# The DeltaNet inverse of a hybrid decoder trunk: fills regrouped, transposes as fills, the last level interleaved

## The reference

```python
A = jnp.where(strict, jnp.einsum('nbhid,nbhjd->nbhij', kb, kc) * decay, 0.0)
T = lax.linalg.triangular_solve(eye + A, jnp.broadcast_to(eye, A.shape), left_side=True, lower=True)
u = T @ vb
w = T @ (kb * jnp.exp(g)[..., None])
...
def step(state, xs):
    v_new = u_i - w_i @ state
    o = (q_i * jnp.exp(g_i)[..., None]) @ state + a_i @ v_new
    ...
```

## Time and profile before

| what | value |
|---|---|
| median of three runs | 1017.67 us (1017.45 to 1018.24) |
| the profiled execution, its own time | 1018.01 us |
| span of its instructions | 1016.2 us |
| PE busy | 1004.5 us (99%) |
| DVE busy | 727.6 us (72%) |
| ACT busy | 602.1 us (59%) |
| POOL busy | 254.7 us (25%) |
| mean granted clock of PE | 0.997 |

### The profile page before, as it was taken

How to read it: one execution, slowest core, us unless ns; L and a number is a source line. 1 busy time by engine, 2 the same in 40 slices (tenths; PEclk the granted TensorE clock), 3 DMA queues, 4 the chain that set the end, 5 groups by cost and what they waited for, 6 DMA issues and landing times.

```text
span 1016.2 us, 19037 instructions
## 1 busy us (share of the span) xinstructions
PE 1004.5 (99%) x6450; PEld 881.3 (87%) x6450; DVE 727.6 (72%) x1206; ACT 602.1 (59%) x1097; POOL 254.7 (25%) x275
## 2 busy tenths in 40 slices
PE   9999999999999999999999999999999999999996
PEld 7888888899988888888888888889999888888885
DVE  5776666899787866666786666668987977666666
ACT  6555555777566655555675555558675575555554
POOL 2767222100520122222202222220016102222221
PEclk9999999999999999999999999999999999999998
DMA  7966666485224666666637666656832338666651
GB/s 230 269 208 201 187 192 193 131 232 165 81 65 125 191 207 192 195 187 188 205 127 223 187 188 194 195 153 170 226 118 64 91 99 272 197 191 188 190 180 42
DMA packets 249882, 176.27 MB, mean 173 GB/s; under 512 B 5875, under 2 KB 235400, under 8 KB 249832
## 3 DMA queue, kind: packets, MB, share of 16 engines
q1 hardware_dynamic: 248800, 174.35, 56.9%
q0 software_dynamic: 400, 0.91, 0.4%
q10 hardware_dynamic: 632, 0.34, 0.1%
HBM read 174.53 MB, written 1.05 MB: 173 GB/s over the span
## 4 chain that ended last, share of the span: by engine, by line
PE 95%; DVE 3%; ACT 1%; issue 0%; DVEq 0%; POOL 0%; POOLq 0%; ACTq 0%
PE bank L800 27%; PE bank L804 14%; PE bank L771 13%; PE bank L772 13%; PE bank L773 13%; PE bank L787 3%; PE bank L790 1%; PE bank L811 1%; PE bank L846 1%; PE bank L1192 1%; PE bank L1179 1%; PE bank L1122 1%; PE bank L853 1%; PE bank L881 0%; PE bank L1104 0%
## 5 line engine op out<-in xcount | busy, mean ns | idle before, releaser
L1894 DVE TENSOR_TENSOR Wl<-raw,Wh 128x1024 fp32r<-128x1024 f32 x324 | 401.8, 1264 | 52.8 <-ACT Wh L1428 52.5
L1428 ACT ACTIVATE Wh<-raw 128x1024 fp32r<-128x1024 f32 x323 | 321.9, 1048 | 19.9 <-PE bank L773 18.0
L800 PE MATMUL bank<-X,Wh 128*128 128x512 f32 x1216 | 288.3, 389 | 0.0
L800 PEld LDWEIGHTS bank<-X,Wh 128*128 128x128 f32 x1216 | 227.9, 188 | 47.2
L623 POOL TENSOR_TENSOR gact<-gact,pooled 128x256 f32<-128x256 f32 x85 | 63.6, 748 | 535.0 <-DVE gact L1993 525.6
L804 PEld LDWEIGHTS bank<-X,Wl 128*128 128x128 f32 x1216 | 153.9, 189 | 5.8
L804 PE MATMUL bank<-X,Wl 128*128 128x256 f32 x1216 | 155.7, 281 | 0.0
L771 PE MATMUL bank<-Wh,aH 128*128 128x512 f32 x336 | 132.4, 394 | 0.2
L772 PE MATMUL bank<-Wl,aH 128*128 128x512 f32 x336 | 131.8, 392 | 0.0
L773 PE MATMUL bank<-Wh,aL 128*128 128x512 f32 x336 | 130.8, 389 | 0.0
L1560 ACT ACTIVATE aH<-hid 128x256 fp32r<-128x256 f32 x84 | 35.1, 418 | 149.1 <-DVE hid L2008 149.1
(11 more groups left out here) (325 smaller groups left out, 1355.6 us busy)
## 6 DMA issues: line engine op xcount, KB each, us to landing
raw<-in_ffn_w_gate SPq DMA_DIRECT2D x88, 512.0 KB, 4.6
raw<-in_ffn_w_up SPq DMA_DIRECT2D x88, 512.0 KB, 3.7
raw<-in_ffn_w_down SPq DMA_DIRECT2D x88, 512.0 KB, 3.3
raw<-in_w_in SPq DMA_DIRECT2D x48, 512.0 KB, 4.8
raw<-in_w_out SPq DMA_DIRECT2D x16, 512.0 KB, 3.3
xr<-in_x SPq DMA_DIRECT2D x2, 512.0 KB, 4.1
out_x<-big SPq DMA_DIRECT2D x3, 256.0 KB, 2.6
cst<-in_consts POOLq DMA_DIRECT2D x1, 688.0 KB, 4.8
```

The lines of the kernel that those rows point to most:

```text
L800: nc.tensor.matmul(b[:, :], piece(Wh, 3 * par + j)[:, k, :], X[:, k, :, :], start=k == 0, stop=False)
L1428: return nc.scalar.activation(Wh[:, s, 0:D_MODEL], raw[:, s, :], ACT.Copy).then_inc(hi_cast.sem, 1)
L1894: return nc.vector.tensor_tensor(low_at(s, skewed), raw[:, s, :], Wh[:, s, 0:D_MODEL].bitcast(F32), ALU.subtract).then_inc(lo_cast.sem, 1)
```

## The change

- PE: the fills are cut at the steps 4, 9, 14, 19 and 24 of the 24 steps. The first four steps come ahead of the first level, the transposes of `VT` come behind it as its fill (now into banks 0 and 1), and five steps each come behind the second, third and fourth level and the quarters. The first level's D no longer waits for the copies of `V`.
- PE: the last level runs as P of half 0, the transposes of q, P of half 1 alternating with D of half 0, the transposes of k, D of half 1. `half_d` reads the diagonal block from `DT`, not from `T64`.
- ACT: the copies of `V` come behind the first level's copies. The edges are written to `DT`, behind DVE's copies of the diagonal blocks. The copy of the pooling input comes ahead of the last level's copies, which alternate with `qT` and `kT`.
- DVE: the 128x4 product and the four copies to `DT` come ahead of the last level. The low cast of piece 27 comes behind the maxima of the first two attention heads.

```diff
-FILL_LEVELS = 2
+FILL_ENDS = (4, 9, 14, 19, 24)
...
-                for c in range(HALVES):
+                def turn_v():
                     pe.wait_ge(*conv_act.at(layer, 12))
-                    pe.wait_ge(*at_done.at(layer, c + 1))
-                    for h in range(DN_HEADS):
-                        m = nc.tensor.transpose(bank[6 + c][:, h * P:(h + 1) * P], VT[:, h, c * P:(c + 1) * P], ident)
-                    m.then_inc(v_turned.sem, 1)
+                    for c in range(HALVES):
+                        for h in range(DN_HEADS):
+                            m = nc.tensor.transpose(bank[c][:, h * P:(h + 1) * P], VT[:, h, c * P:(c + 1) * P], ident)
+                        m.then_inc(v_turned.sem, 1)
...
-                def turn_qk():
+                def turn_qk(j):
                     pe.wait_ge(*roped.at(layer, 4))
-                    for j in range(2):
...
+                    pe.wait_ge(*v_copied.at(layer, j + 1))
...
+                def fill(first, last):
+                    for step in range(first, last):
+                        n, k = divmod(step, KT)
...
                     pe.wait_ge(*pm_done.at(layer, 2 * n + c + 1))
-                    if n == 0:
-                        pe.wait_ge(*v_copied.at(layer, c + 1))
-                    else:
+                    if n:
                         pe.wait_ge(*dt_done.at(layer, 2 * (n - 1) + c + 1))
...
+                def half_level():
+                    pe.wait_ge(*d_done.at(layer, 8 + 1))
+                    for h, u in units(0):
+                        m = half_p(h, u)
                     m.then_inc(p_done.sem, 1)
+                    turn_qk(0)
+                    pe.wait_ge(*d_done.at(layer, 8 + 2))
+                    pe.wait_ge(*pm_done.at(layer, 10 + 1))
+                    pe.wait_ge(*dt_edge.at(layer, 1))
+                    for (h, u), (_, v) in zip(units(0), units(1)):
+                        p = half_p(h, v)
+                        d = half_d(h, u)
+                    p.then_inc(p_done.sem, 1)
+                    d.then_inc(dd_done.sem, 1)
+                    turn_qk(1)
+                    pe.wait_ge(*pm_done.at(layer, 10 + 2))
+                    pe.wait_ge(*dt_edge.at(layer, 2))
+                    for h, u in units(1):
+                        m = half_d(h, u)
                     m.then_inc(dd_done.sem, 1)
...
+                fill(0, FILL_ENDS[0])
                 for n in range(len(LEVELS)):
...
+                    if n == 0:
+                        turn_v()
+                    else:
+                        fill(FILL_ENDS[n - 1], FILL_ENDS[n])
+                for stage in (quarter_p, quarter_d):
+                    for c in range(HALVES):
+                        stage(c)
+                fill(FILL_ENDS[3], FILL_ENDS[4])
+                half_level()
...
-                    nc.scalar.activation(T64[0:32, u, 32:64], src[0:32, :, :], ACT.Copy)
-                    nc.scalar.activation(T64[64:96, u, 32:64], src[64:96, :, :], ACT.Copy).then_inc(dt_edge.sem, 1)
+                    act.wait_ge(*dt_joined.at(layer, c + 1))
+                    nc.scalar.activation(DT[0:32, u, 32:64], src[0:32, :, :], ACT.Copy)
+                    nc.scalar.activation(DT[64:96, u, 96:128], src[64:96, :, :], ACT.Copy).then_inc(dt_edge.sem, 1)
                 z_silu(3)
                 act.preload_act_table_set(LN_EXP)
+                pool_raw(0)
                 for c in range(HALVES):
+                    act.wait_ge(*qk_turned.at(layer, c + 1))
+                    nc.scalar.activation((qT, kT)[c][:, :, :].rearrange("p a t -> p (a t)"), bank[c][:, :],
+                                         ACT.Copy).then_inc(qk_copied.sem, 1)
                     act.wait_ge(*dd_done.at(layer, 10 + c + 1))
...
+                small(nc.vector.tensor_tensor(beta_dec, beta_k[:, 0:4], dec[:, 0:4, P - 1:P].rearrange("p u t -> p (u t)"),
+                                              ALU.mult))
+                dve.wait_ge(*cleared.at(layer, 1))
+                for c in range(HALVES):
+                    u = slice(4 * c, 4 * c + 4)
+                    dve.wait_ge(*dt_done.at(layer, 6 + c + 1))
+                    for q in BLOCKS:
+                        op = nc.vector.tensor_copy(DT[q, u, q], T64[q, u, :])
+                    op.then_inc(dt_joined.sem, 1)
                 for c in range(HALVES):
                     dve.wait_ge(*p_done.at(layer, 10 + c + 1))
...
                 lo_mix(layer, 26)
-                lo_mix(layer, 27)
...
                 maxima(1)
+                lo_mix(layer, 27)
```

More of the change, by code:

```diff
@@ L1136, in mixer @@
                 pe.wait_ge(*at_done.at(layer, 4))
-                def turn_qk():
+                def turn_qk(j):
                     pe.wait_ge(*roped.at(layer, 4))
-                    for j in range(2):
[L1142 to L1156, removed]
-                    else:
-                        pe.wait_ge(*pool_x.at(layer, 1))
-                    for k in ks:
+                    pe.wait_ge(*v_copied.at(layer, j + 1))
@@ new lines, in turn_qk @@
+                    for c in range(HALVES):
+                        for pair in range(2):
+                            m = nc.tensor.transpose(bank[j][:, pair * SEQ + c * P:pair * SEQ + (c + 1) * P],
+                                                    qkr[:, c, j * 256 + pair * P:j * 256 + (pair + 1) * P], ident)
+                    m.then_inc(qk_turned.sem, 1)
+                def fill(first, last):
+                    for step in range(first, last):
+                        n, k = divmod(step, KT)
+                        pos, out = FILL_POSITIONS[n], bank[(3, 2, 3)[n]][:, 0:SEQ]
+                        s = MIX_SLOTS[pos]
+                        if step == first or k == 0:
+                            split(pos)
+                            if pos == POS_POOL1:
+                                pe.wait_ge(*diff_done.at(layer, 2))
+                            elif pos == POS_Z3:
+                                pe.wait_ge(*z_act.at(layer, 3))
+                            else:
+                                pe.wait_ge(*pool_x.at(layer, 1))
@@ L1160, in fill_part @@
                         m = three(out, piece(Wh, s)[:, k, :], low_piece(s)[:, k, :], Xh[:, k, :], Xl[:, k, :],
                                   k == 0, k == KT - 1)
-                    if ks[-1] == KT - 1:
-                        m.then_inc(proj.sem, 1)
+                        if k == KT - 1:
+                            m.then_inc(proj.sem, 1)
                 def units(c):
@@ L1218, in quarter_d, with half_p @@
                     m.then_inc(dd_done.sem, 1)
[L1220 to L1225, removed]
-                    m.then_inc(p_done.sem, 1)
[L1228 to L1234, removed]
+                def half_p(h, u):
+                    return nc.tensor.matmul(bank[4 + u // DN_HEADS][HALF:, h * HALF:(h + 1) * HALF], LT[0:HALF, u, HALF:],
+                                            D64[0:HALF, u, :], start=True, stop=True)
@@ new lines, in half_d @@
+                def half_d(h, u):
+                    return nc.tensor.matmul(bank[6 + u // DN_HEADS][0:HALF, h * HALF:(h + 1) * HALF], PM[HALF:, u, 0:HALF],
+                                            DT[HALF:, u, HALF:], start=True, stop=True)
+                def half_level():
+                    pe.wait_ge(*d_done.at(layer, 8 + 1))
+                    for h, u in units(0):
+                        m = half_p(h, u)
+                    m.then_inc(p_done.sem, 1)
+                    turn_qk(0)
[12 more added lines that the diff above has]
+                        m = half_d(h, u)
@@ L1235, in half_d @@
                     m.then_inc(dd_done.sem, 1)
+                fill(0, FILL_ENDS[0])
                 for n in range(len(LEVELS)):
-                    k = 4 * (n % 2)
                     for stage in (level_p, level_d):
@@ L1315, in mixer @@
                 pe.wait_ge(*dt_edge.at(layer, 3))
-                pe.wait_ge(*dt_joined.at(layer, 1))
                 pe.wait_ge(*pm_done.at(layer, 2 * N_LEVELS))
@@ L1325, in mixer @@
                 pe.wait_ge(*dt_edge.at(layer, 4))
-                pe.wait_ge(*dt_joined.at(layer, 2))
                 pe.wait_ge(*vd_done.at(layer, 1))
@@ L1747, in mixer @@
                 z_silu(2)
[L1748 to L1752, removed]
                 for n, s in enumerate(LEVELS):
@@ L1758, in mixer @@
                         nc.scalar.activation(even, src, ACT.Copy).then_inc(d_done.sem, 1)
+                    if n == 0:
+                        act.wait_ge(*q_summed.at(layer, 2))
+                        for c in range(HALVES):
+                            act.wait_ge(*v_turned.at(layer, c + 1))
+                            nc.scalar.activation(V[:, 4 * c:4 * c + 4, :].rearrange("p u d -> p (u d)"), bank[c][:, :],
+                                                 ACT.Copy).then_inc(v_copied.sem, 1)
                     act.wait_ge(*k_norm.at(layer, 1))
@@ L1763, in mixer @@
```

(4 more changed lines are left out.)

## The result

The changed kernel takes 1019.17 us (median of 20 runs, 1018.28 to 1019.75), the kernel before 1017.43 us beside it (20 runs, 1016.79 to 1018.24): ratio 1.0016, 95% interval 1.0011 to 1.0022. It is slower, by 1.7 us and not by the 4.0 of the forecast. That is within the 0.2% that the forecast called no change, but the interval tells it from no change all the same. The profiled execution took 1018.93 us, with a span of 1017.1 us.

What follows compares the result with a forecast made beforehand. PE was taken as busy nearly throughout, so its work and new waits decide. Per layer +1.5 ahead of T and +0.5 behind, twice +2.0 is +4.0 on 1018.01, less 0.34 for the median: 1021.7 us, range 1017.6 to 1023.2.

Steps and rivals of the forecast that it cites:

- First level, -0.20: First level of the inverse on PE: D no longer waits for V's copies, 1.25 becomes 1.05 us behind P.
- PE's own order in full: PE's work in the inverse, if nothing else holds it: first product with DT at 288.06 instead of 288.36.
- +0.86: Quarters on PE: 19 fill steps ahead instead of 16 make them 1.06 us later, less 0.20 from the first level.
- -0.1: Last level on PE: three blocks of 0.79, 2.37 us, against 2.45 before; bounds -0.3 to +0.4.
- T: Start of the first product that uses the finished inverse DT, at 288.36 us in layer 0 of the kernel before.
- The middle block's 0.60: Last level on PE: alternating P and D run together as pairs, in the time of one half, 0.60 us.
- The way of the blocks to DT, +1.8 on top of that: DVE's copies wait for POOL's steps, three waits of 0.6; T at 289.9, +1.5 per layer against before (-0.3 to +2.3).
- the small product, 0.57: DVE's small product between the quarters' negations and the copies to DT: claimed to take 0.57 us.
- ACT from the last copy to T, 3.8: ACT's edges, activation, table load, pooling copy, qT and DT block: 3.71 us, about 3.8 with a semaphore.
- A copy waits for POOL: DVE's copies to DT: each waits for the POOL step it meets, and POOL's next step for it; at most 2.6 us.
- Behind T, +0.5: Low cast of piece 27 behind the maxima: L2378 0.8 us later, 0.3 absorbed, 0.5 per layer carried on (bounds 0 and 0.8).
- the first rival: Copies to DT run beside POOL unhindered: T at 288.1, +0.24 per layer, 1018.2 us; chance 0.22.

Runs made afterwards that it cites:

- the run with POOL held: Changed kernel with POOL's first windows made to wait until DVE's four copies to DT are done: 1017.98 us, ratio 1.0007.
- the run with the cast alone: Kernel before with only the low cast of piece 27 moved behind the maxima: 1018.58 us, ratio 1.001.

## Why the prediction was wrong

The mechanism was right and its size was not. By its steps:

- *First level, -0.20.* Right: 1.05. PE's own order in full was under-priced: -0.3 forecast, -0.51 shown by the run with POOL held. Part of it lies in the levels: the quarters' first product stands 23.12 behind the Gram product in that run and 22.36 before, +0.76 in place of +0.86. The rest, -0.21 in place of -0.1, lies between there and T. None of this reached T in the changed kernel, where ACT decided. The middle block's 0.60 was right (0.61).
- *The way of the blocks to DT, +1.8 on top of that.* This is the step that failed. It put T at 289.9, and on the time axis of the trace before T came at 288.67 (257.56 + 0.69 + 30.42 = 288.67), 1.2 earlier. I laid two chains of estimates end to end, and each was too long:
  - the small product, 0.57 by the earlier trace rows, took 0.15. The 0.57 was not its price. In the trace before it stands beside POOL's first step of the second windows, 288.21 to 289.39, and ends with it at 289.42; in the run with the cast alone, where POOL is idle beside it, it takes 0.16. I read a duration with a wait in it as a price: 0.4.
  - the copies, 1.21 with three waits of 0.6, 3.0; they took 2.66, three waits of about 0.5: 0.35.
  - DVE started on the quarters 0.1 earlier (281.87 on that axis, 281.95 in the sum), as PE did.
  - ACT from the last copy to T, 3.8; it took 3.48. From start to start the pooling copy takes 0.28 and not 0.44, a distance that I had read in the earlier trace rows where qT came later, and qT takes 0.48 and not 0.60, which was its duration: 0.3.

  Together about 1.2, all on the same side. The signs named for the mechanism came: POOL's first windows end at 285.06 (285.75 on that axis; 285 to 286 foretold), and T waits for ACT's block.
- *A copy waits for POOL.* Right, and shown: 0.29 in every run in which POOL is idle beside it, 0.73 to 0.80 for the three behind the first in the changed kernel. By the Trainium skill ("SBUF — State Buffer", Who interferes with whom) a copy in a two-port mode and a GpSimd instruction exclude each other for a whole instruction, and the trace agrees. The prediction called this a rule against its part, but it is the same mechanism. The same section says it of DVE instructions with two inputs in SBUF beside a GpSimd instruction that reads SBUF, as the small product and POOL's step are; that sentence, held against the 0.57 of the earlier trace rows, would have spoken against my price.
- *Behind T, +0.5.* Right: +0.43, and +0.42 for the cast alone. R1 comes 0.75 later behind T (5.76 in place of 5.01; 0.8 forecast).
- *Sum.* 0.31 and 0.43 a layer in place of 1.5 and 0.5. The forecast of over 0.2% rested on the failed step alone; without it the first rival's 1018.2 was nearer than the forecast, though not for its reason, since the copies are not free.

POOL's step beside the small product, in the trace before:

```profile
288.21 1.18 POOL L712 TENSOR_TENSOR win_a<-win_x 128x256 f32<-128x256 f32 x1 [5.46 <-ACT win_x L1659]
```

## What to carry to other kernels

Before a duration is used as a price, look at what ran beside that record: a DVE copy within SBUF, or a DVE instruction with two inputs there, can have a wait in it when POOL is busy. Sum a chain of one engine from start to start, and look whether those starts had something else to wait for. Work moved on one engine moves its partners' collisions: here one group of transposes moved on PE shifted POOL by 3.7 us, and what helped was to put it back, to place one of DVE's casts where POOL is idle and to take the other out of the chain behind T.

## What the runs showed that was not expected

- The starts of the records do not tell which of DVE and POOL goes first: with POOL's record 0.03 ahead of DVE's in both layers, the cast went first in one and POOL in the other, 0.46 apart in what followed.
- A small instruction waits too: a 128x4 product took 0.57 beside POOL's step in the kernel before, and 0.15 in the run with POOL held.
- Two kernels that differ only in where DVE's casts stand can differ by 3.7 us in the median (1016.95 and 1020.65), of which the traces explain 1.1.
